# Two-layer encoder trunk on one core: a first half step taken row tile by row tile, and a sum of squares folded on VectorE

## What is computed

```python
def rms_norm(x, w):
    xf = x.astype(jnp.float32)
    y = xf * lax.rsqrt(jnp.mean(xf * xf, axis=-1, keepdims=True) + RMS_EPS)
    return (y * w.astype(jnp.float32)).astype(x.dtype)
...
        h = rms_norm(x, mixer_norm_w[layer])
        if layer % 2 == 0:
            proj = h @ hyb_w_in[j]
```

## Time and profile before

| | |
|---|---|
| median of 3 runs | 2092.64 us (2091.36 to 2093.26) |
| profiled execution | 2091.34 us, span 2089.3 us |
| TensorE matmuls busy | 2080.0 us, 100% of the span |
| VectorE busy | 1217.6 us, 58% |
| ScalarE busy | 973.5 us, 47% |
| DMA | 447 MB moved, 214 GB/s mean |

### The profile page before, as it was taken

One profiled execution on the slowest core, in us unless ns is written; L12 is line 12 of the kernel. 1 busy time (PEld: TensorE's weight loads), 2 busy tenths in 40 slices (PEclk: granted clock), 3 DMA queues, 4 the chain that ended last, 5 costly groups with the idle time before them and its releaser, 6 DMA issues.

```text
span 2089.3 us, 22670 instructions
## 1 busy us (share of the span) xinstructions
PE 2080.0 (100%) x9420; PEld 1723.5 (82%) x9420; DVE 1217.6 (58%) x1298; ACT 973.5 (47%) x1086; POOL 149.8 (7%) x251
## 2 busy tenths in 40 slices
PE   9999999999999999999999999999999999999999
PEld 8877888888888888888888888888888888888887
DVE  7776655555455554556666666656555465554654
ACT  6556554443444434445555455554443444434443
POOL 1010100100001000011110100100100001000010
PEclk9999999999999999999999999999999999999999
DMA  9665776765667656677766666766766567665673
GB/s 334 215 184 180 240 238 207 232 219 194 197 206 232 219 194 198 205 234 245 239 212 206 213 201 197 232 216 217 238 209 201 187 213 238 209 201 187 213 237 129
DMA packets 214566, 447.37 MB, mean 214 GB/s; under 512 B 10224, under 2 KB 10240, under 8 KB 214208
## 3 DMA queue, kind: packets, MB, share of 16 engines
q1 hardware_dynamic: 197600, 392.72, 56.2%
q0 software_dynamic: 16448, 51.08, 9.3%
q10 hardware_dynamic: 416, 2.13, 0.3%
HBM read 419.67 MB, written 26.21 MB: 213 GB/s over the span
## 4 chain that ended last, share of the span: by engine, by line
PE 96%; DVE 2%; ACT 2%; issue 0%; DVEq 0%; POOL 0%; POOLq 0%
PE acc L1087 31%; PE acc L1093 31%; PE acc L1088 31%; DVE w_lo L742 1%; ACT att L653 1%; ACT w_hi L539 0%; PE turn_zb L1206 0%; PE turn_zb L1233 0%; PE turn_zb L1107 0%; PE turn_zb L1146 0%; DVE att L968 0%; DVE att L953 0%; DVE p_folded L791 0%; PE turn_zb L1117 0%; ACT L511 0%
## 5 line engine op out<-in xcount | busy, mean ns | idle before, releaser
L742 DVE TENSOR_TENSOR w_lo<-raw,w_hi 128x1024 fp32r<-128x1024 f32 x744 | 899.5, 1220 | 591.6 <-ACT w_hi L539 591.4
L539 ACT ACTIVATE w_hi<-raw 128x1024 fp32r<-128x1024 f32 x744 | 786.1, 1059 | 982.9 <-PE acc L1093 978.5
L1087 PE MATMUL acc<-w_hi,xT_hi 128*128 128x512 f32 x2016 | 788.1, 391 | 0.7 <-ACT w_hi L539 0.6
L1088 PE MATMUL acc<-w_hi,xT_lo 128*128 128x512 f32 x2016 | 785.8, 390 | 0.0
L1093 PE MATMUL acc<-w_lo,xT_hi 128*128 128x512 f32 x2016 | 539.3, 390 | 0.7 <-DVE w_lo L742 0.7
L1087 PEld LDWEIGHTS acc<-w_hi,xT_hi 128*128 128x128 f32 x2016 | 379.1, 188 | 81.4 <-issue 1.8
L1093 PEld LDWEIGHTS acc<-w_lo,xT_hi 128*128 128x128 f32 x2016 | 378.5, 188 | 79.8 <-DVE w_lo L742 1.5
L1088 PEld LDWEIGHTS acc<-w_hi,xT_lo 128*128 128x128 f32 x2016 | 379.3, 188 | 77.2
L1087 PE MATMUL acc<-w_hi,m_hi 128*128 128x512 f32 x960 | 374.3, 390 | 0.0
L1088 PE MATMUL acc<-w_hi,m_lo 128*128 128x512 f32 x960 | 373.9, 389 | 0.0
L1093 PE MATMUL acc<-w_lo,m_hi 128*128 128x512 f32 x960 | 256.7, 389 | 0.0
(11 more groups left out here) (149 smaller groups left out, 526.5 us busy)
## 6 DMA issues: line engine op xcount, KB each, us to landing
raw<-in_w_gate SPq DMA_DIRECT2D x88, 1024.0 KB, 5.2
raw<-in_w_up SPq DMA_DIRECT2D x88, 1024.0 KB, 5.9
raw<-in_w_down SPq DMA_DIRECT2D x88, 1024.0 KB, 5.1
raw<-in_w_qkv SPq DMA_DIRECT2D x48, 1024.0 KB, 5.8
raw<-in_w_out SPq DMA_DIRECT2D x32, 1024.0 KB, 5.2
raw<-in_w_in SPq DMA_DIRECT2D x26, 1024.0 KB, 6.1
blocks<-folded POOLq DMA_DIRECT2D x42, 512.0 KB, 4.0
spread<-blocks POOLq DMA_DIRECT2D x168, 128.0 KB, 6.0
```

What stands on the lines that cost most here:

```text
L539: nc.scalar.activation(w_hi[:, h.slot, :, :], raw[:, h.raw_slot, 2 * h.part:2 * h.part + 2, :], ACTF.Copy).then_inc(hi_ready, 1)
L742: nc.vector.tensor_tensor(w_lo[:, h.slot, :, :], raw[:, h.raw_slot, 2 * h.part:2 * h.part + 2, :], f32(w_hi[:, h.slot, :, :]), ALU.subtrac ...
L1087: nc.tensor.matmul(dst, hi[:, h.k0 + k, at], wh, start=h.opens and k == 0, stop=False)
L1088: nc.tensor.matmul(dst, lo[:, h.k0 + k, at], wh, start=False, stop=False)
```

## The change

It has two parts that do not touch each other.

**Half 0 by row tile.** The first piece of x is cut in two pieces of one row tile, and the first half unit of weights in two loads of one row tile (128 x 512). ScalarE rounds x's row tile 0, then the weights' row tile 0, then those of row tile 1. TensorE takes the eight matmuls with `w_hi` of half 0 in the order of the row tiles, each as soon as its own tile is there. SyncE issues two more loads than before.

**The sum of squares.** At t = 8 VectorE adds the upper half of the 1024 columns onto the lower (128 x 512), waits for it, and adds once more (128 x 256). TensorE at t = 9 waits for that and has 2 matmuls in place of 8.

```diff
-XT_PIECES = [0, 2, 4, 6, 8, 12, KT]
-PIECE_AT = {0: 0, 1: 1, 2: 2, 3: 3, 4: 4, 6: 5}
+XT_PIECES = [0, 1, 2, 4, 6, 8, 12, KT]
+PIECES_AT = {0: (0, 1), 1: (2,), 2: (3,), 3: (4,), 4: (5,), 6: (6,)}
...
+                if u == 0:
+                    for q in range(2):
+                        load_x(q)
+                        sp.dma_start(raw[:, u, q:q + 1, :], src[:, q:q + 1, :]).then_inc(first_landed[q], 16)
+                    load_x(2)
+                    sp.dma_start(raw[:, u, 2:4, :], src[:, 2:4, :]).then_inc(raw_landed[u], 16)
+                    return
                 if u < 4:
-                    load_x(u + min(u, 2))
-                if u in (0, 1):
-                    sp.dma_start(raw[:, u, 0:2, :], src[:, 0:2, :]).then_inc(first_landed[u], 16)
-                    load_x(2 * u + 1)
+                    load_x(u + 2 + (u > 1))
+                if u == 1:
+                    sp.dma_start(raw[:, u, 0:2, :], src[:, 0:2, :]).then_inc(half_landed, 16)
+                    load_x(4)
                     sp.dma_start(raw[:, u, 2:4, :], src[:, 2:4, :]).then_inc(raw_landed[u], 16)
                     return
...
+                    if piece < 2:
+
+                        act.wait_ge(first_landed[piece], 16)
+                        nc.scalar.activation(w_hi[:, 0, piece, :], raw[:, 0, piece, :], ACTF.Copy).then_inc((first_hi, hi_ready)[piece], 1)
+                if h.index == 0:
+                    return
...
+                if t == 8:
+
+                    dve.wait_ge(xt_summed, 3)
+                    s = xt_squares[0]
+                    link(nc.vector.tensor_tensor(s[:, 0:2 * SEQ], s[:, 0:2 * SEQ], s[:, 2 * SEQ:], ALU.add))
+                    nc.vector.tensor_tensor(s[:, 0:SEQ], s[:, 0:SEQ], s[:, SEQ:2 * SEQ], ALU.add).then_inc(xt_summed, 1)
...
+                if h.index == 0:
+
+                    for k in range(2):
+                        pe.wait_ge((first_hi, hi_ready)[k], 1)
+                        pe.wait_ge(xt_lo, k + 1)
+                        for tt in range(TT):
+                            dst, at = acc[:, it.pair(h.c), tt, :], slice(tt * P, (tt + 1) * P)
+                            nc.tensor.matmul(dst, hi[:, k, at], w_hi[:, 0, k, :], start=k == 0, stop=False)
+                            nc.tensor.matmul(dst, lo[:, k, at], w_hi[:, 0, k, :], start=False, stop=False)
+                    pe.wait_ge(lo_ready, 1)
...
-                    pe.wait_ge(xt_summed, 3)
+                    pe.wait_ge(xt_summed, 4)
                     pe.wait_ge(cleared, 2)
                     for tt in range(TT):
-                        for k in range(4):
-                            at = k * SEQ + tt * P
-                            ins = nc.tensor.matmul(zb[:, tt * CH:tt * CH + 1], xt_squares[0][:, at:at + P], ones_sb[:, 0:1],
-                                                   start=k == 0, stop=k == 3)
+                        ins = nc.tensor.matmul(zb[:, tt * CH:tt * CH + 1], xt_squares[0][:, tt * P:(tt + 1) * P], ones_sb[:, 0:1],
+                                               start=True, stop=True)
```

More of the change, by code:

```diff
@@ L336, in build @@
         first_landed = [sem(f"first_landed{u}") for u in range(2)]
+        half_landed = sem("half_landed")
+        first_hi = sem("first_hi")
         nw_landed = sem("nw_landed")
@@ L521, in half @@
             def half(it, h):
-                if h.index in PIECE_AT:
-                    piece = PIECE_AT[h.index]
+                for piece in PIECES_AT.get(h.index, ()):
                     act.wait_ge(xt_landed[piece], 16)
@@ L530, in half @@
                     ins.then_inc(xt_hi, 1)
-                if h.index in (0, 2):
-                    act.wait_ge(first_landed[h.unit], 16)
+                    if piece < 2:
[3 more added lines that the diff above has]
+                    return
+                if h.index == 2:
+                    act.wait_ge(half_landed, 16)
                 elif h.part == 0 or h.index in (1, 3):
@@ L1060, in stationary_ready @@
                 if n == 0:
-                    if h.s in PIECE_AT:
-                        pe.wait_ge(xt_lo, PIECE_AT[h.s] + 1)
+                    for piece in PIECES_AT.get(h.s, ()):
+                        pe.wait_ge(xt_lo, piece + 1)
                     return
@@ L1076, in half @@
                 hi, lo = lhs(ph)
+                if h.index == 0:
[7 more added lines that the diff above has]
+                    pe.wait_ge(lo_ready, 1)
+                    for tt in range(TT):
+                        dst, at = acc[:, it.pair(h.c), tt, :], slice(tt * P, (tt + 1) * P)
+                        for k in range(2):
+                            ins = nc.tensor.matmul(dst, hi[:, k, at], w_lo[:, 0, k, :], start=False, stop=False)
+                        ins.then_inc(products_done, 1)
+                    return
                 if it.i == 0 and h.c == 0:
```

## The result

The changed kernel takes 2094.02 us (median of 22 executions, 2092.64 to 2096.69) against 2091.36 us for the kernel before in the same sessions (22 executions, 2089.81 to 2093.4). The ratio is 1.0013, with a 95% interval of 1.0007 to 1.0019: slower by 2.7 us, which is inside the 0.2% that I had called no change. 0.5 us had been forecast. The profiled execution took 2094.01 us, with a span of 2092.0.

A forecast was written before the change was run, and what follows sets the result against it. TensorE was taken as the bound, its matmuls filling 2080.0 of 2089.3 us. The terms 0 + 0 - 1.27 + 1.74 gave +0.5 us, a median of 2093.1 us, range 2090.9 to 2095.7.

The forecast's parts named there:

- That TensorE's row of products is set by half 4: First 40 us: unit 2's landing sets half 4 at 17.76 us, so half 0 by row tile brings 0.
- Two more loads: SyncE's first loads: unit 2 issued some 0.96 us later, its landing set by bytes; 0, between -0.55 and +0.96 us.
- rival C: DMA queue at the start: it runs thin and the whole 0.96 us shows, 2094.1 us; chance 8%.
- The matmuls removed: TensorE's sum of squares before half 9: 12 of 16 records go, at 0.106 us each, -1.27 us.
- the wait added: TensorE before half 9: waits for VectorE's two adds behind half 10's split, 33.22 instead of 31.48 us, +1.74 us.
- Rival A: Sum of squares: VectorE has the folded sum by 31.5 us, the 1.27 us are kept, 2091.4 us; chance 10%.
- Rival B: TensorE behind the new wait: the granted clock falls as well, costing 0.46 + 1.6 us, 2094.7 us; chance 25%.
- Who is behind the waits: Later splits, `var` and first chunk's reading: no one on TensorE's path waits for them; 0, up to 0.85 us otherwise.

The follow-up runs named there:

- the fold alone: Kernel before with only VectorE's two adds at t = 8 and TensorE's 2 matmuls at t = 9; 2094.42 us against 2091.41, ratio 1.0012.
- the filled fold: Kernel before with the two adds and 2 matmuls, plus 6 matmuls on ones ahead of TensorE's wait; 2091.79 us against 2091.51, ratio 1.0001.
- the weights cut alone: Changed kernel without the sum-of-squares part, x's first piece whole, weights' first half unit cut in two loads; 2092.01 us against 2091.51, ratio 1.0006.
- the run that asks one half later: Kernel before with the two adds at t = 8 and TensorE's 2 matmuls at t = 10; 2091.38 us against 2091.41, ratio 1.0003.
- the two small loads: Kernel before with loads of 8 and 4 KB moved from GpSimd's queue to SyncE's, behind x's first piece; 2092.33 us against 2091.51, ratio 1.0007.
- the later gap filled: Kernel before with 8 matmuls on ones in TensorE's 2.33 us idle at 142 us; 2094.14 us against 2091.48, ratio 1.0012.

## Why the prediction was right or wrong

*That TensorE's row of products is set by half 4, and that what is gained before it is lost there:* right. The first product moved by 0.03 us (6.67), within the 0.15 given, and half 4 came after an idle, of 0.29 us. One reading in it was wrong without harm: ScalarE's start did move, from 4.35 to 3.28 us, and then ScalarE waited 0.98 us for the weights of row tile 1, so that `w_hi` was complete at 6.92 us and not at 6.50.

```profile
3.28 0.51 ACT L537 ACTIVATE xT_hi<-xT_raw,normw_sb 128x256 fp32r<-128x256 f32 x1 [0.81 <-DMA normw_sb<-in_normw]
...
6.29 0.63 ACT L542 ACTIVATE w_hi<-raw 128x512 fp32r<-128x512 f32 x1 [0.98 <-DMA raw<-in_w_in]
```

*Two more loads: 0, between -0.55 and +0.96.* This is the term that failed. It measured 1.51 us in the profiled execution, and 1.12 as the mean of three profiles against seven, and the upper bound was too low for both. I had argued that bytes set the landing, since over 3 MB had been issued by 6.2 us and the queue could not be empty. From 4 to 6 us, which I had not looked at, the engines of the changed kernel moved 194 GB/s at a share of 0.75, and those of the kernel before 380 at 1.01. Of after, and then of before:

```profile
4.00:6.00 2.00, 2.00 (x11) 2.00 (x11) 0.79 (x2) 1.11 (x2) 0.00 (x0) 1.00 0.75 194
```

```profile
4.00:6.00 2.00, 2.00 (x13) 2.00 (x13) 0.71 (x2) 1.47 (x3) 0.00 (x0) 1.00 1.01 380
```

That is 0.37 MB, worth 0.95 us at 393 GB/s, and it isn't made up (253 against 285 GB/s over the first 12 us): rival C, the loads run thin, was what happened, and it explains 0.95 of the 1.5 us; the rest is open. The place was wrong too. I had reckoned with the issue of unit 2, 0.96 us later. It went out 1.97 us later, since the issues ahead of it took 0.67 to 1.08 us from 4.5 us on and not 0.48; but half 2, whose weights were issued 0.91 us later, was already 1.52 us late, and half 4 was 1.50 late on ScalarE, so the lateness of unit 2's own issue didn't show. Why SyncE's issues stretch there isn't settled; they do so in the kernel before as well, somewhat later.

*The matmuls removed, -1.27, and the wait added, +1.74:* the net was to be +0.46. It measured 0.43 in the change, 0.44 and 0.43 in the fold alone and the filled fold. The parts agree too: the adds took 0.69 and 0.43 us (0.68 and 0.42 from rows of the same shapes), and the idle came to 1.54 us. In the prediction's own terms TensorE's sum started 1.66 us later behind half 4 (15.38 against 13.72) where 1.74 was forecast, and its 4 records took 0.47 where 0.42 was; the two misses are small and of opposite sign. Rival A, that the gain shows, fell with it.

*Rival B, the clock as well, 25%.* It was likelier than that. By the granted clock, in 7 of 11 executions of the fold alone the mean was lower than in any of the 33 of the kernel before; filling the gap took this away. No profile caught the fall at this wait (from 33 to 38 us the granted clock is 1.00 in the profiles of the change and of the fold alone), so its place is inferred from the filler, and its price, some 2 us on average for the fold alone, from the clock's means. That it depends on more than the length of the idle is plain in the later one. It is 2.33 us long in the profile of the weights cut alone as in that of before, but there the 16 records and the products behind ran at full pace (145.57 to 147.35 is 1.78 us; before it was 2.41):

```profile
145.57 2.02 PE L1174 MATMUL turn_zb<-gs,wsT 128*128 128x128 f32 x16 [2.33 <-DVE m_lo L794]
147.35 0.48 PE L1115 MATMUL acc<-w_hi,xT_hi 128*128 128x512 f32 x1
147.66 0.40 PE L1116 MATMUL acc<-w_hi,xT_lo 128*128 128x512 f32 x1
```

So the same wait is sometimes paid twice and sometimes once (the clock fell there in 9 of the 11 profiles in which it isn't filled), and one profile of one execution is no proof that it is free. The fold alone had the shortest of its 11 executions profiled. In the profile of the weights cut alone the clock fell elsewhere: TensorE waited 2.02 us for `xT_lo` near 1005 us, at the place of the changed kernel's 0.6, and the stretch behind has 0.53.

```profile
1004.93 0.65 PE L1115 MATMUL acc<-w_hi,xT_hi 128*128 128x512 f32 x1 [2.02 <-DVE xT_lo L814]
1005.38 0.63 PE L1116 MATMUL acc<-w_hi,xT_lo 128*128 128x512 f32 x1
```

```profile
1004.90:1008.50 3.60, 3.56 (x9) 2.79 (x10) 2.01 (x7) 3.24 (x5) 2.33 (x4) 0.53 0.39 114
```

*Who is behind the waits: 0.* Right for the change. It holds only because TensorE itself was late: in the run that asks one half later, TensorE waits 1.17 us for k.

The sum, with sizes as measured: 1.12 for the loads and 0.44 for the wait leave 1.1 of the 2.66 us. The clock accounts for about that: its mean over the 22 executions was 0.9987 (7 at 0.998, 14 at 0.999, 1 at 1.000), against 0.9993 to 0.9995 for the kernel before beside the experiments, which is 1.1 to 1.5 us from values that are rounded to 0.001. The 0.6 us near 1000 us is chance, as far as single profiles tell: waits there or up to 60 us behind were between 0 and 2.0 us in the others, in kernels with either part of the change and with neither. The point forecast of 2093.1 against 2094.02 looks better than it is, since it stood on a first median of 2092.64, and 22 executions put that kernel at 2091.36. The forecast was a change of 0.5 us, and it was 2.7: the result lies in the range because the range had room for the loads and for one fall of the clock.

What stays open: the executions of 2096 us and more, at 0.998, of the kernels that cut half 0 or its loads, of that with the two small loads and of the kernel before with the later gap filled. The wait near 1005 us is a candidate: 2.0 us of wait and 1.6 for a fall, on top of an execution of 2092.2 with the other fall, make 2095.8 (an estimate from these figures), and the seven at 0.998 of the fold alone, at 2093.4 to 2095.7, don't need it. No such execution was profiled, so it isn't shown, nor why it should come in those kernels and in none of the 99 executions of the kernel before. Open too is how much of the loads' slip is the issue and how much the queue.

## What to carry to other kernels

A matmul that is taken off the engine that bounds the kernel is worth nothing if what replaces it ends later on an engine that is full in that stretch: follow the new producer's place in its queue, and then the next thing that hangs on its result. Cutting the first loads finer costs their issues, and everything queued behind them pays (1.1 us for two more here), while what they serve may be waiting for something else anyway. Where TensorE has to wait for a microsecond or two, look at the granted clock of many executions and not at one profile, and try matmuls on nothing in the gap.

## What the runs showed that I had not expected

A gap of 1.5 us in TensorE's work cost 0.44 us in the trace and 3.0 us in the median, and with 6 useless matmuls in it the median was 0.3 us above the kernel before. In the one profile with two more loads of 12 KB together, ahead of megabytes, half 4 started 0.8 us later than in the mean of the seven without, and later than in any of them. In the changed kernel the whole slip was there at half 2, before unit 2's turn.
